# One placement modulo 256 bytes for all four weight ring slots, and no token reversal

## The reference, cut to what matters

```python
D_MODEL, D_FF = 2048, 5632
def swiglu(x, w_gate, w_up, w_down):
    return (jax.nn.silu(x @ w_gate) * (x @ w_up)) @ w_down

proj = xn @ w_in                                   # input projection of the three mixers
out = jnp.concatenate([o_gla, o_conv, o_cm], axis=-1) @ w_out
xp = xp + hp
xp = xp + swiglu(rmsnorm(xp, norm2_g[l]), w_gate[l], w_up[l], w_down[l])
```

## Time and profile before

| what | value |
|---|---|
| median of 3 runs | 2194.41 us |
| the profiled execution, time of its run | 2195.34 us |
| its span, first to last instruction | 2193.6 us |
| TensorE busy | 2180.9 us, 17357 matmuls |
| VectorE busy | 1710.7 us (78%) |
| ScalarE busy | 1002.8 us (46%) |
| matmuls of L1619 | 11 groups of 1056 or 528, 11088 in all |
| matmuls of L1302 | 3 groups of 1280, 3840 in all |
| matmuls of L1526, L1518, L1564 | 756, 288, 672 |

### The profile page before, as it was taken

One profiled execution on the slowest core, in us unless ns is written; L12 is line 12 of the kernel. 1 busy time (PEld: TensorE's weight loads), 2 busy tenths in 40 slices (PEclk: granted clock), 3 DMA queues, 4 the chain that ended last, 5 costly groups with the idle time before them and its releaser, 6 DMA issues.

```text
span 2193.6 us, 41269 instructions
## 1 busy us (share of the span) xinstructions
PE 2180.9 (99%) x17357; PEld 2172.2 (99%) x17357; DVE 1710.7 (78%) x1987; ACT 1002.8 (46%) x1331; POOL 9.6 (0%) x15
## 2 busy tenths in 40 slices
PE   9999999999999999999999999999999999999998
PEld 9999999999999999999999999999999999999998
DVE  7765478546796788888887888888888888787887
ACT  7333523224454554444444544444444545444455
POOL 0000000000000000000000000000000000000000
PEclk9999999999999999999999999999999999999999
DMA  5232324245333425445445444444545876555523
GB/s 190 94 108 87 102 72 145 79 128 187 129 105 103 155 98 171 134 142 166 141 133 165 141 131 156 154 130 142 166 141 168 301 280 222 186 205 192 187 83 116
DMA packets 121516, 325.51 MB, mean 148 GB/s; under 512 B 10699, under 2 KB 51211, under 8 KB 120364
## 3 DMA queue, kind: packets, MB, share of 16 engines
q1 hardware_dynamic: 120860, 323.69, 43.9%
q10 hardware_dynamic: 528, 0.07, 0.0%
HBM read 267.09 MB, written 56.63 MB: 148 GB/s over the span
## 4 chain that ended last, share of the span: by engine, by line
PE 97%; DVE 1%; issue 1%; ACT 1%; DMA 0%; SPq 0%; POOLq 0%; POOL 0%; DVEq 0%; ACTq 0%
PE acc L1619 36%; PE g L1619 26%; PE acc L1302 21%; PE acc L1526 2%; PE acc L1564 2%; PE g L1526 2%; PE g L1564 2%; PE g L1518 1%; PE acc L1518 1%; PE g L1329 0%; PE g L1452 0%; DMA trunk<-xT 0%; PE g L1459 0%; PE g L1351 0%; PE g L1466 0%
## 5 line engine op out<-in xcount | busy, mean ns | idle before, releaser
L1123 ACT CAST w_hi<-w_s 128x1024 fp32r<-128x1024 f32 (+1 forms) x204 | 209.1, 1025 | 358.8 <-DVE w_s L2413 350.5
L1619 PE MATMUL acc<-op_hi,w_hi 128*128 128x272 f32 x1056 | 304.8, 289 | 0.4 <-ACT acc L1097 0.4
L1619 PE MATMUL g<-op_hi,w_hi 128*128 128x272 f32 x1056 | 304.5, 288 | 0.0
L1619 PE MATMUL acc<-op_hi,w_lo 128*128 128x272 f32 x1056 | 304.4, 288 | 0.0
L1619 PE MATMUL acc<-sg_hi,w_hi 128*128 128x272 f32 x1056 | 304.4, 288 | 0.0
L1619 PE MATMUL acc<-op_lo,w_hi 128*128 128x272 f32 x1056 | 304.3, 288 | 0.0
L1619 PE MATMUL acc<-sg_lo,w_hi 128*128 128x272 f32 x1056 | 304.2, 288 | 0.0
L1619 PE MATMUL g<-op_lo,w_hi 128*128 128x272 f32 x1056 | 304.2, 288 | 0.0
L1619 PE MATMUL acc<-sg_hi,w_lo 128*128 128x272 f32 x1056 | 304.1, 288 | 0.0
L1619 PE MATMUL g<-op_hi,w_lo 128*128 128x272 f32 x1056 | 304.0, 288 | 0.0
L1302 PE MATMUL acc<-op_hi,w_hi 128*128 128x272 f32 x1280 | 267.9, 290 | 0.0
(11 more groups left out here) (390 smaller groups left out, 5001.1 us busy)
## 6 DMA issues: line engine op xcount, KB each, us to landing
w<-w_gu SPq DMA_DIRECT2D x88, 512.0 KB, 3.3
w_raw<-w_gu SPq DMA_DIRECT2D x88, 512.0 KB, 3.9
w_raw<-w_in SPq DMA_DIRECT2D x64, 512.0 KB, 3.5
hf_dram<-hf_hi SPq DMA_DIRECT2D x22, 952.0 KB, 6.5
hf_dram<-hf_lo SPq DMA_DIRECT2D x22, 952.0 KB, 8.8
w_raw<-w_d SPq DMA_DIRECT2D x32, 512.0 KB, 4.4
w<-w_d SPq DMA_DIRECT2D x26, 512.0 KB, 3.3
op_hi<-hf_dram SPq DMA_DIRECT2D x16, 544.0 KB, 7.0
```

The lines of the kernel that those rows point to most:

```text
L1123: nc.scalar.copy(w_hi[:, (C_ST + n) % RING, 0:w], src[:, 0:w]).then_inc(hi_ready, 1)
L1619: last = nc.tensor.matmul(out, w, x, start=fresh and j == 0 and i == 0, stop=j == h - 1 and i == 2, skip_group_check=True)
```

## The change

All four slots of each ring become 4096 bytes long without a gap, starting 16 bytes into the tensor, so every slot starts at 144 (upper) or 208 (lower) modulo 256, which is where slot 1 started before. The tensors keep their size (4 x 1028 columns), so all that follows them stays where it was. The reversal of `idx` 2 and 5 is removed, on the token operands and on the output. Nothing else differs: the same instructions, waits and DMAs.

```diff
-BACKWARD = (2, 5)
...
-        w_hi = sb("w_hi", [P, RING, CH + SHIFT], F32R)[:, :, 0:CH]
-        w_lo = sb("w_lo", [P, RING, CH + SHIFT], F32R)[:, :, 0:CH]
+        w_hi = sb("w_hi", [P, RING * CH + 4 * SHIFT], F32R)[:, SHIFT:SHIFT + RING * CH].rearrange("p (r c) -> p r c", r=RING)
+        w_lo = sb("w_lo", [P, RING * CH + 4 * SHIFT], F32R)[:, SHIFT:SHIFT + RING * CH].rearrange("p (r c) -> p r c", r=RING)
...
                     out = banks[idx][:, q, 0:TH]
-                    if idx in BACKWARD:
-                        out = out[:, ::-1]
...
                         x_h, x_l = form_hi[idx][:, e + j, :], form_lo[idx][:, e + j, :]
-                        if idx in BACKWARD:
-                            x_h, x_l = x_h[:, ::-1], x_l[:, ::-1]
```

## The result

The changed kernel takes 2205.57 us, the median of 6 runs (2204.74 to 2206.63), against 2194.59 us before (6 runs, 2194.23 to 2196.99): a ratio of 1.0046 with a 95% interval of 1.0036 to 1.0056. It is slower by about 11 us. The prediction was 2188.7 us, 2186 to 2193.

A forecast was written before the change was run, and what follows sets the result against it. The prediction took the rate at which one TensorE matmul follows another as the bound. Gains of 3.7 + 0.2 + 1.5 + 0.3 = 5.7 us gave 2189.6 us for the profiled execution, 2188.7 us for the median, range 2186.0 to 2193.0.

The forecast's parts named there:

- The bound: Whole kernel: only the rate at which one TensorE matmul follows another sets the time; TensorE busy 2180.9 of 2193.6 us.
- the splits' write times: Splits on ScalarE and VectorE write to other addresses beside TensorE's work; costed at nothing.
- the price of gate, up and down: 11088 matmuls, counted as 462 products of 24, go from 3.012 to 3.004 us each, gaining 3.7 us.
- bounds of 3.000 and 3.010: Product times in gate, up and down: 3.000 gives 2186.1 us in all, 3.01 gives 2192.6 us.
- The 56 products of 18 matmuls: In down: priced like the products of 24, by matmul count, inside the 3.7 us gain.
- Removing the reversal: Gate, up and down: products 2 and 5 go from 3.02 or 3.01 to 3.004 us, inside the 3.7 us.
- The output projection's products: 28 products in the output projection go from a mean of 3.010 us to 3.004, gaining 0.2 us.
- The chunks: 80 chunks of 48 matmuls go from 6.02 to 6.00 us each; 1.6 us, counted as 1.5.
- k and v: 1044 matmuls in k and v gain between 0 and 0.8 us; 0.3 us taken.
- Rival (C): One placement locks weight and token streams into a bad alignment in every product: 3.025 us each, 2200.8 us; chance 0.05.
- (A): One placement's steady rhythm is worse than its first 24 matmuls: 3.007 to 3.012 a product, 2190.1 to 2194.4 us; chance 0.22.
- (B): Placement and direction do nothing in themselves, so the time stays at 2194.4 us; chance 0.07.

The follow-up runs named there:

- the five placements: Changed kernel (144/208) and four with rings moved to 128/192, 160/224, 176/240 or 144/192, one placement throughout, all forward: 2205.57, 2198.39, 2196.92, 2196.20, 2200.79 us.
- the kernel at 176 and 240: Changed kernel with all slots moved to 176 (upper) and 240 (lower) modulo 256, tokens unmoved, all forward: 2196.20 us in one execution.
- the staggered kernel: Kernel before, its four placements kept, with every gate, up, down and output projection product reversed: 2188.44 us in one execution.
- the one with the best of each stage: Changed kernel with gate, up, down and output projection products reversed, k and v and chunks forward: 2188.02 us, ratio 0.9969 to the kernel before.

## Why the prediction was wrong, step by step

**The bound was read rightly.** TensorE's distance of starts sets the time, nothing waits, and the splits' write times don't matter (ScalarE 1001.6 and VectorE 1709.5 us busy).

**The step that failed** is the price of gate, up and down: "I stay at 3.004, a mean of what was seen". Five products of slot 1 were taken for the rate of a kernel that has nothing else, with -3.7 us; a product of 24 measured 3.040, and the stage came to +10.9 us (8.22 and 2.65). The text had named the gap, that in the rows such a product always follows one of another slot, and then closed it with bounds of 3.000 and 3.010 taken from the same passing products and from the chunks. A product of 24 matmuls is only two turns of a 12-matmul rhythm, and in the output projection it took 48 matmuls to settle; a product of slot 1 between others could not show it. The 56 products of 18 matmuls, priced alike by count, did gain the 0.3 us of their share. The chunks in slot 1 had settled, but on another sequence of rows, and the five placements show that one doesn't rank the other. A smaller slip: the prediction speaks of four forward products in slot 1 in these 28, and there are five. Number 111 takes 3.01 us (1118.73 to 1121.74), which makes the mean 3.005 and changes nothing in the argument.

**Removing the reversal** was counted as a gain and was, with staggered placements, worth 0.02 us in 84.34, which is nothing. With one placement it was the last thing that broke the slow rhythm.

**The output projection's products** went from -0.2 to +0.63 us for the same reason.

**The chunks** were right in kind: 6.00 us in all slots of the output projection. They gave back 1.1 us where 1.5 were counted; as the prediction had feared, the waits among those of the input projection took a part. **k and v** gave 0.07 instead of 0.3, within the bounds of 0 and 0.8.

**Rival (C) is what happened**, by its mechanism: one placement locks the streams into a bad alignment in every product of 24. I gave it 0.05, at 3.025 a product and 2200.8 us, because all slow rates stood in slot 0 and "none is in slot 1, whose placement is kept". It came out at 3.040, over any product's rate in the rows: a mean over passing alignments bounds nothing about the one that stays. (A) had the right doubt with a size too small: 3.012 at most. (B) fell: 16 bytes move a whole stage by 8 us. The Trainium skill's "TensorE: Matmul & The Clock Gate" gives TensorE two independent read ports, so that a weight load takes no read bandwidth from the running matmul (section on what each phase is for). The runs here don't agree in so far as the place of the weights against the tokens moves the forward rate between 3.013 and 3.040 us a product; whether that happens at a port or in the memory behind it no run shows.

**What stays open** is why a given relation of placement, row sequence and direction yields the value it does. That it is a repeating rhythm, what ends it, and that it depends on these three is shown; the rule behind the value is not, nor why the kernel at 176 and 240 has two of them. Nor is it shown what in the direction does it: each reversal turned the read of the tokens and the write to PSUM together, and neither was turned alone.

## What to carry to other kernels

When matmuls follow each other with no wait and products of equal work still differ in time, try the start of the weight and token buffers in steps of 16 bytes and the direction of the stream, stage by stage; neither adds an instruction, and here together they were worth 0.3% one way and 0.5% the other. Judge a placement only by a kernel that keeps it long enough to settle, not by the rate that single products show between others: the best in passing was the worst in the long run. Two edits that each measure as nothing in a stage can together cost the whole difference, so test both alone and both together before one is dropped as useless.

## What the runs showed of the hardware that wasn't expected

The settled rates come in steps. With one placement throughout, 24 matmuls of 272 tokens take 3.000, 3.013, 3.027 or 3.040 us, and 48 in chunks 6.000, 6.027 or 6.053: 1500.0, 1506.7, 1513.3 and 1520.0 ns for 12 matmuls. The step of 6.67 ns is 16 cycles of 2.4 GHz, worked out from these values, and no value between was seen for products of 24 or chunks in the middle of a stage. None of these is under 125.0 ns a matmul, though passing products in the staggered kernel reach 2.991. But that is no floor: products of 18 matmuls, which have three token rows in turn instead of four, settle at 2.240 us when reversed (124.4 ns a matmul), at 2.253 or 2.267 forward in the other placements. These are the same steps, for 9 matmuls: 1120.0, 1126.7 and 1133.3 ns.

A stretch of half clock, PEclk 0.51 in the window above, begins near 228 us in 8 of 14 profiled executions and lasts 3.4 or 6.8 us. It starts during eight matmuls of 33 partitions by 512, which take 3.7 us where the clock stays up, or within 0.5 us after them; the window above that runs into them has 84 matmuls in 12 us. In the kernel before and in five others it is absent, in equal code, so it belongs to the execution and not to the kernel: in the one with the best of each stage the same window holds 84 matmuls too, and the clock stays at 1.00.
